# Prompt indexer: the weighted relu of the four heads summed by TensorE through diagonal weights, VectorE takes the sum one head later

## What is computed

```python
def index_scores(qi, wi, ki):
    dots = jnp.einsum('bqhd,bsd->bqhs', qi, ki) * (IDX_DIM ** -0.5)
    return jnp.einsum('bqh,bqhs->bqs', wi, jax.nn.relu(dots)).astype(jnp.float32)
...
    score = index_scores(qi_b, wi_b, ki)
    score = jnp.where(kpos[None, None, :] <= qpos[None, :, None], score, -jnp.inf)
    _, top_i = lax.top_k(score, topk)
```

## Time and profile before

| | |
|---|---|
| median of 3 runs | 4307.72 us (4307.31 to 4313.46) |
| profiled execution, its own time | 4309.53 us |
| its span, first to last instruction | 4307.9 us |
| PE busy | 3640.4 us, 85% |
| PE weight loads | 2742.6 us, 64% |
| DVE busy | 2136.8 us, 50% |
| ACT busy | 1029.1 us, 24% |
| mean granted clock of TensorE | 0.871 |

### The profile page before, as it was taken

The page is one execution under the profiler, slowest core; times in us unless marked ns, Lnnn a source line. Parts: engine busy times, 40 slices in busy tenths (PEclk is TensorE's granted clock), DMA queues, the critical chain, the costliest instruction groups (busy, mean ns, idle before and its releaser), DMA issues.

```text
span 4307.9 us, 52606 instructions
## 1 busy us (share of the span) xinstructions
PE 3640.4 (85%) x17978; PEld 2742.6 (64%) x17978; DVE 2136.8 (50%) x4900; ACT 1029.1 (24%) x2273; POOL 476.8 (11%) x639
## 2 busy tenths in 40 slices
PE   6778878787578999999987777886885789999999
PEld 3545555454334999999854545554543359999997
DVE  1357778834613333443423677787355234344334
ACT  2333333214311121112123323332152011111110
POOL 0100000022200000000101000000222001100001
PEclk9888888558789999999998988785587899999999
DMA  4000000173521111111310000001745211111111
GB/s 129 21 13 13 13 11 8 30 81 108 176 96 54 41 48 40 40 40 59 134 42 21 13 15 14 10 8 35 77 135 177 76 55 40 40 40 42 56 40 52
DMA packets 192447, 230.68 MB, mean 54 GB/s; under 512 B 82962, under 2 KB 152660, under 8 KB 192180
## 3 DMA queue, kind: packets, MB, share of 16 engines
q1 hardware_dynamic: 163300, 159.40, 13.8%
q0 software_dynamic: 21600, 57.08, 4.2%
q10 hardware_dynamic: 7280, 10.83, 0.7%
HBM read 203.74 MB, written 23.50 MB: 53 GB/s over the span
## 4 chain that ended last, share of the span: by engine, by line
PE 67%; DVE 15%; issue 8%; ACT 4%; DVEq 3%; POOLq 1%; DMA 1%; POOL 1%; ACTq 0%
PE bank L1306 12%; PE bank L1307 12%; PE bank L1308 12%; PE bank L1016 10%; DVE arena L1367 6%; PE bank L1012 5%; PE bank L1114 4%; PE bank L1298 3%; PE bank L1098 2%; ACT arena L645 1%; DVE arena L1634 1%; PE bank L1106 1%; PE bank L1202 1%; PE bank L1060 1%; DVE vectors L1371 1%
## 5 line engine op out<-in xcount | busy, mean ns | idle before, releaser
L1776 DVE TENSOR_TENSOR x_rows<-x_rows,bank 128x512 f32<-128x512 f32 (+1 forms) x576 | 396.2, 688 | 629.0 <-PE bank L1308 629.0
L645 ACT ACTIVATE arena<-bank 128x512 f32<-128x512 f32 (+11 forms) x926 | 348.0, 428 | 856.5 <-PE bank L1016 313.8
L1016 PE MATMUL bank<-arena 128*128 128x512 f32 (+5 forms) x1440 | 520.8, 517 | 3.2 <-ACT arena L673 1.5
L1367 DVE TENSOR_SCALAR_CACHE_REDUCE arena<-arena,vectors 128x384 bf16<-128x384 f32 (+6 forms) x434 | 500.0, 1152 | 34.3 <-issue 2.5
L1306 PE MATMUL bank<-xT_hi,w_up_hi 128*128 128x364 f32 (+1 forms) x1536 | 506.9, 330 | 3.2 <-DVE vectors L1757 3.2
L1307 PE MATMUL bank<-xT_lo,w_up_hi 128*128 128x364 f32 (+1 forms) x1536 | 506.9, 330 | 0.0
L1308 PE MATMUL bank<-xT_hi,w_up_lo 128*128 128x364 f32 (+1 forms) x1536 | 506.8, 330 | 0.0
L1306 PE MATMUL bank<-w_down_hi,hidden_hi 128*128 128x512 f32 x1152 | 449.8, 390 | 7.5 <-issue 7.5
L1307 PE MATMUL bank<-w_down_lo,hidden_hi 128*128 128x512 f32 x1152 | 449.4, 390 | 0.0
L1308 PE MATMUL bank<-w_down_hi,hidden_lo 128*128 128x512 f32 x1152 | 449.3, 390 | 0.0
L1016 PEld LDWEIGHTS bank<-arena 128*128 128x128 f32 (+1 forms) x1440 | 252.6, 193 | 251.0 <-issue 221.9
(11 more groups left out here) (248 smaller groups left out, 4399.4 us busy)
## 6 DMA issues: line engine op xcount, KB each, us to landing
w_up_landing<-in_w_up SPq DMA_DIRECT2D x32, 1024.0 KB, 7.5
w_down_landing<-in_w_down SPq DMA_DIRECT2D x32, 1024.0 KB, 4.9
arena<-in_cache_k SPq DMA_DIRECT2D x128, 128.0 KB, 2.7
arena<-in_cache_k POOLq DMA_DIRECT2D x128, 128.0 KB, 2.9
arena<-in_cache_v SPq DMA_DIRECT2D x128, 128.0 KB, 2.9
arena<-in_cache_v POOLq DMA_DIRECT2D x128, 128.0 KB, 2.9
arena<-in_w_in ACTq DMA_DIRECT2D x4, 2048.0 KB, 16.1
arena<-in_cache_ki SPq DMA_DIRECT2D x256, 32.0 KB
```

What stands on the lines that cost most here:

```text
L645: return act.activation(dst, src, ACT.Copy, scale=scale)
L1016: ins = mm(b[:R, o:o + w], xnT[:, c, 0:R], w_in[:, c, c0:c0 + w], start=c == 0, stop=c == 7)
L1367: ts(junk, sc, cf[:R].bitcast(F32), None, ALU.is_ge, ALU.add, accum_out=cnt[:R])
L1776: tt(x, x, b[P - R:P, :], ALU.add).then_inc(s_took, 1)
```

## The change

For each chunk PE now does the weighting and the sum. DVE builds, in slot 3 of each step, four diagonal matrices `dw` (the identity times the head's weight per query, 128 x 128 each, in the place of `sq`). After the four dots of a chunk PE multiplies each `dw` with its relu and accumulates the four products in one of DVE's banks (float32, 128 rows, as many columns as the chunk has keys). ACT may write a relu once PE has used the one two before it. DVE copies the sum from the bank to `score`, adding the bias on the way to the last 128 columns, and does so right behind `head_max` of the next head (slots 5 and 6 instead of 4 and 5), ahead of that slot's search bits. `plan()` gets the two new uses of a DVE bank.

```diff
--- before.py
+++ after.py
@@ -78,6 +78,8 @@
             for h in range(9):
                 if h < 8 and A_ is not None:
                     dve += [(l, A_, f"qk{h}.{c}") for c in range(len(chunks(width(A_))))]
+                if h in (5, 6) and 2 <= s < NT and h - 5 < len(chunks(width(s))):
+                    dve.append((l, s, f"is{h - 5}"))
                 if h == 1:
                     if attends(s - 1) is not None:
                         act.append((l, A_ - 1 if A_ is not None else NT - 1, "yb"))
@@ -194,7 +196,7 @@
     for l in range(DEPTH):
         for t in range(2, NT):
             IDX0[l, t] = i
-            i += 4 * len(chunks(width(t)))
+            i += len(chunks(width(t)))
     ctx = ExitStack()
     with ctx, nc.allow_non_contiguous_dma(reason="short vectors and states, element by element"):
         vectors = ctx.enter_context(nc.sbuf_tensor("vectors", [P, 288], F32))
@@ -259,6 +261,7 @@
         gcol, normw, glanw, convw, vecs, bd, wa2, axs, rl = zone(E0, ARENA, gcol=8, normw=(2, 64), glanw=64, convw=(4, 2), vecs=16, bd=(2, 2, P), wa2=P, axs=(2, 8, 11), rl=(2, 512))
         junk = junk.bitcast(mybir.dt.bfloat16)
         rt = view(sq.rearrange("p a b -> p (a b)")[:, 0:544], (4, 136))
+        dw = view(sq.rearrange("p a b -> p (a b)")[:, 0:512], (4, P))
         osq = sq.rearrange("p a b -> p (a b)")[:, 512:768]
 
         SsBDa, SsBDb = view(score[:, 2, :], (4, 4, 64)), view(xnT.rearrange("p a b -> p (a b)"), (4, 4, 64))
@@ -337,7 +340,7 @@
         s_thr, s_ln, s_E, s_tg = sem("gates_ready"), sem("logs_ready"), sem("decays_ready"), sem("tanh_ready")
         s_q, s_AT, s_S = sem("gla_operands"), sem("gla_attn_ready"), sem("gla_state_ready")
         s_ossq, s_ors, s_yc, s_ya = sem("gla_out_squares"), sem("gla_out_rstd"), sem("yc_ready"), sem("ya_ready")
-        s_idx = sem("relu_used")
+        s_idx, s_dw = sem("relu_summed"), sem("diag_w")
         s_nb, s_p, s_pv, s_yb = sem("max_ready"), sem("probs_ready"), sem("pv_done"), sem("yb_ready")
         s_out = sem("stored")
         s_wi, s_wis, s_msk, s_nbs, s_ps, s_pvs, s_os = (sem("diag_wi"), sem("wisel_ready"), sem("sample_mask"), sem("smax_ready"),
@@ -798,12 +801,17 @@
 
                 def index_relu(t, c):
                     w = chunks(width(t))[c][1]
+                    n = IDX0[l, t] + c
                     for i in range(4):
-                        k = IDX0[l, t] + 4 * c + i
-                        if k >= 2:
-                            act.wait_ge(s_idx, k - 1)
+                        if i == 1 and n:
+
+                            before = (l, t, f"is{c - 1}") if c else (l, t - 1, f"is{len(chunks(width(t - 1))) - 1}") if t > 2 else (l - 1, NT - 1, "is1")
+                            act.wait_ge(s_full_d, D_AT[before] + 1)
+                        elif i != 1:
+                            if n or i:
+                                act.wait_ge(s_idx, 3 * n + (0, 0, 1, 2)[i])
                         b = take((l, t, f"i{c}.{i}"))
-                        act.activation(rl[:, k % 2, 0:w], b[:, 0:w], ACT.Relu, scale=0.125).then_inc(s_evac, 1)
+                        act.activation(rl[:, i % 2, 0:w], b[:, 0:w], ACT.Relu, scale=0.125).then_inc(s_evac, 1)
 
                 def exp(t, h):
                     act.wait_ge(s_nb, (l * NT + t) * 8 + h + 1)
@@ -1059,6 +1067,12 @@
                         j = i % 2
                         mm(b[:, 0:w], QiT[64 * j:64 * j + 64, i // 2, :], kiT[64 * j:64 * j + 64, c0:c0 + w],
                            start=True, stop=True).then_inc(s_full_a, 1)
+                    if c == 0:
+                        pe.wait_ge(s_dw, l * (NT - 2) + t - 1)
+                    b4 = d_bank((l, t, f"is{c}"))
+                    for i in range(4):
+                        evac((l, t, f"i{c}.{i}"))
+                        mm(b4[:, 0:w], dw[:, i, :], rl[:, i % 2, 0:w], start=i == 0, stop=i == 3).then_inc(s_idx if i < 3 else s_full_d, 1)
 
                 def gla_attention(t):
                     R = rows(t)
@@ -1549,21 +1563,21 @@
                             ins = cp(SsBDb[k, :, h, :], Ss[k, 4:8, :])
                     ins.then_inc(s_q, 1)
 
+                def diag_weights(t):
+                    for i in range(4):
+                        ins = ts(dw[:, i, :], ident, wca[:, t % 2, i:i + 1], None, ALU.mult)
+                    ins.then_inc(s_dw, 1)
+
                 def index_scores(t, c):
                     c0, w = chunks(width(t))[c]
-                    for i in range(4):
-                        v.wait_ge(s_evac, A_AT[l, t, f"i{c}.{i}"] + 1)
-                        src, dst = rl[:, (IDX0[l, t] + 4 * c + i) % 2, 0:w], score[:, t % 3, c0:c0 + w]
-                        wi = wca[:, t % 2, i:i + 1]
-                        if i == 0:
-                            ts(dst, src, wi, None, ALU.mult).then_inc(s_idx, 1)
-                        else:
-                            stt(dst, src, wi, dst, ALU.mult, ALU.add).then_inc(s_idx, 1)
-                        D_()
-                    if c == len(chunks(width(t))) - 1:
-                        d = score[:, t % 3, t * P:(t + 1) * P]
-                        tt(d, d, cs("bias"), ALU.add)
-                        D_()
+                    b = take((l, t, f"is{c}"))
+                    n = w - P if c == len(chunks(width(t))) - 1 else w
+                    if n:
+                        ins = cp(score[:, t % 3, c0:c0 + n], b[:, 0:n])
+                    if n < w:
+                        ins = tt(score[:, t % 3, t * P:(t + 1) * P], b[:, n:w], cs("bias"), ALU.add)
+                    ins.then_inc(s_took, 1)
+                    D_()
 
                 def all_keys(t):
                     if t:
@@ -1648,6 +1662,8 @@
                     for h in range(8):
                         if A_ is not None:
                             head_max(A_, h)
+                        if h in (5, 6) and 2 <= s < NT and h - 5 < len(chunks(width(s))):
+                            index_scores(s, h - 5)
                         if T_ is not None and h == 0:
                             top_sign(sc, P, jk)
                         if h == 0 and P_:
@@ -1669,13 +1685,13 @@
                         if h == 3 and P_:
                             gate_sums(s)
                             recurrence(s)
+                            if 2 <= s < NT:
+                                diag_weights(s)
                         if h == 4:
                             if P_:
                                 gla_operands(s)
                             if s < 2:
                                 all_keys(s)
-                        if h in (4, 5) and 2 <= s < NT and h - 4 < len(chunks(width(s))):
-                            index_scores(s, h - 4)
                         if h == 6 and P_:
                             gla_mask(s)
                         if h == 7 and P_:
```

## The result

The changed kernel takes 4358.98 us (median; 4351.84 to 4365.78), the kernel before 4308.72 us beside it: ratio 1.0115, interval 1.0096 to 1.0133. That is slower by 50 us; the forecast was 4366, the range 4343 to 4391. The profiled execution took 4357.53 us, its span is 4355.5.

What follows compares the result with a forecast made beforehand. PE was taken to bound each step from slot 3 or 4 to `gla_out`, DVE from there to the next step's slot 1. Sums of 60.6 us less 2.5 given back made 58 us more: 4366 us, range 4343 to 4391.

Steps and rivals of the forecast that it cites:

- the added matmuls: PE's sums behind each chunk's dots, steps 2 to 7: priced by line 1016's 0.865 us per 512 columns, 60.6 us together.
- A wait that goes away: PE's wait before head 6's values, step 7, slot 7: delayed PE work fills it, giving back 1.4 + 1.1 us.

Runs made afterwards that it cites:

- before_again: The kernel before, unchanged, run and profiled again on the chip of some experiments: 4310.32 us, ratio 1.0002.
- before_dense9: The kernel before with five wide matmuls on PE at the end of step 8 and two ahead of each head's logits (heads 1 to 7) in step 9: 4295.58 us.

## What to carry to other kernels

Moving work from a half-idle engine to a busy one pays only if the half-idle one sets the end of the stretch in which the work lies; read that from who waits at the next meeting point (here `gla_out`), and not from the busy share. Price the added matmuls by a row of the same rows, columns and type in an unbroken stretch: that was right within 1 us in 60. A wait that goes away can be worth more than its length where the clock falls behind it (4.3 us for 1.4 in the first layer here). Where a change does two things, the part that moves the work to another place can be the gain: here DVE's adding one head later without PE's sums gives 11 us (4297.1; the larger part of it lies in steps that it does not touch). Two wide matmuls per head in step 9, with the five in step 8, give 12.5 (4295.58). Both beat the two kernels, and they were not run together.

## What the runs showed of the hardware

- PE without a pause was not PE at 2.4 GHz. In step 9, with matmuls of 64 columns or 64 rows in good part, a head takes 9.02 us at 1.2 GHz; with two matmuls of 128 rows by 512 columns more it takes 6.44. The clock of steps 8 to 10 rose from 0.56 to 0.66:

```profile
777.30:984.90 207.60, 147.87 (x544) 103.04 (x542) 115.17 (x342) 46.49 (x107) 36.39 (x54) 0.56 0.45 58
```

```profile
777.70:978.10 200.40, 143.72 (x582) 95.31 (x580) 115.18 (x341) 46.54 (x107) 36.37 (x54) 0.66 0.45 60
```

  (before_again, then before_dense9, which does more work on PE and is busy for less time).
- The profiles of one kernel differ by some 3 us in single steps although the totals agree within 0.3%; in steps 3 and 7 the longer ones have the lower mean clock (89.1 us at 0.89 and 93.2 at 0.84 in step 3). So a part of a change under 5 us should be read from several steps and both layers.
